# The second up tile of the gated MLP done plainly, and the borders of the MLP stage reordered

## The chip, the cores and the metric

One NeuronCore of one Trainium2 chip runs the whole layer in one launch. The metric is the device time in microseconds (us) of that launch; lower is better. Engines: TensorE (PE, matmuls), VectorE (DVE), ScalarE (ACT), GpSimd (POOL) and SyncE (SP, which here only issues DMAs). Each has a queue of its own that it works off in order; they wait for each other by semaphores.

## The reference

Two groups of tokens (512 and 1024, so 1536 columns) pass through one encoder layer in float32: RMSNorm, one input projection, two kinds of attention, output projection, a gated MLP with a convolution of width 3, a gated embedding, a final RMSNorm. The change touches the border from the output projection to the MLP, the MLP, and the border from its up to its down projection:

```python
h = h + mixed @ w_out[i]
n2 = _rmsnorm(h, ffn_norm[i])
u = _dwconv_centred(n2 @ w_up[i], conv_w[i], conv_b[i])   # up[:, :-2]*w[0] + up[:, 1:-1]*w[1] + up[:, 2:]*w[2] + bias
a, g = jnp.split(u, 2, axis=-1)
h = h + (a * jax.nn.gelu(g, approximate=True)) @ w_down[i]
```

D_MODEL is 1024, D_FF 2816. `w_up` is 1024 x 5632, `w_down` 2816 x 1024.

## The kernel before

Activations lie transposed: features on the 128 partitions, the 1536 tokens along the free axis, in G = 3 groups of 512 columns. `H` holds the residual stream as KT = 8 pieces of 128 features. A float32 product is done in three passes: each operand is split into a rounded high half (`NH`, `WH`, `AH`, by ScalarE) and the rest (`NL`, `WL`, `AL`, by VectorE), and `three_pass` (L317) multiplies high x high, high x low and low x high into one PSUM bank. So each k step of 128 features against 512 tokens is three matmuls of 128x512.

**Stage 3, output projection** (`s3_*`, L1484 to L1757). Eight output tiles, each for three groups. VectorE merges the two halves of a tile's result into `H` (`merge`, L1687: four instructions), ScalarE squares it, GpSimd adds the square to `rstd_h` (L1517). For the last tile this closes the norm of a group: `norm_sums` on PE, `group_std` on ScalarE, `group_recip` on VectorE, `norm_row` on PE, a copy by ScalarE into `rstd_h`; after that VectorE multiplies each of the 24 pieces (8 features x 3 groups) by gain and norm (`normed`, L1737), ScalarE rounds it (`high`, L1653), VectorE makes the low half (`low`, L1742). The weights of the first up tile are split before `last_merge(0)`.

**Stage 4, MLP** (`s4_*`). The 22 tiles j of 128 up columns have a content and a gate half each.

- Tile 0 is done plainly on PE, piece by piece, while the pieces are being made: 6 matmuls per piece, with `WH`, `WL`, `gate0_h`, `gate0_l`.
- Tiles 1 to 21 use a Strassen-Winograd scheme on quarters of the content and gate weights (`A11`, `A21`, `A22`, `A12`, 128x512 each, loaded by `load_quarter`) against group 1 and 2, and a plain one for group 0: `PRODUCTS` (L1771) lists 11 products of 12 matmuls, 132 a tile. It needs sums of weight quarters (`weight_sum`, GpSimd, L1897; rounded by `sum_high`, `sum_low`) and four sets of four combinations of pieces of x (GpSimd, L1920, in the order 1, 3, 2, 4; rounded by `combo_high`, L2060, and `combo_low`, L2190, which write into `NH`, `NL` and over `H`). The combinations are made once, piece by piece, as soon as the pieces of group 2 are there. The product P4 of tile 1 is the first that reads them. `combine` (L2219) and `copy` (L2070) put the products together in `u_a` and `u_g`.
- Per tile: `centre` (ScalarE, L2083: middle tap and bias), `taps` (VectorE, L2202: four instructions per half), `gelu` (ScalarE, L2088), `product` (VectorE, L2208), `store_act` (SP: the tile's result to DRAM). The loop of SP has the loads of the next tile's quarters and the store in one order: A21, store of tile j-1, A11, A22, A12.
- The down projection runs three groups x 22 tiles; a tile is 24 matmuls. `down_high` (L2129, L2130) and `down_low` (L2252, L2255) split weights and activations of a tile. `load_down` and `load_act` load them two tiles ahead, as each buffer comes free. At the end of a group VectorE adds the result to `H` (L2279), ScalarE squares it, GpSimd sums; after that all eight pieces are rounded (`NH`, L2170) and their low halves made (`rest`, L2273) for stage 5, before tile 2 of the next group is split. The embedding's input `pT` and two weight tiles (`PLE_raw`) are loaded right before the loads of tile 4 of group 0, and eight loads of `H` follow tiles 5, 7, ... 19.

Of the kernel before, what the change touches and what calls it, by code (L numbers as in the profile page):

```python
# [105 lines left out]
def build(nc, a):  # L106
    ctx = ExitStack()
    with ctx:
# [134 lines left out]
        S_first = over("S_first", X0, [2, GT], F32, 26 * KB)  # L243
# [1360 lines left out]

        def s3_scalar(act):
# [67 lines left out]
            high(1, range(6, KT))  # L1673
            high(2, range(KT))

        def s3_vector(dve):
# [45 lines left out]
            split_lo(dve, FF0, 0)  # L1722
            dve.wait_ge(w_hi, FF0 + 2)
            for half in range(2):
                low = nc.vector.tensor_tensor(gate0_l[half][:], raw[:, 1, cols(half)], gate0_h[:, cols(half)].bitcast(F32), ALU.subtract)
                if half:
                    low.then_inc(w_lo, 1)

            def last_merge(g):
                last_out_ready(dve, g)  # L1730
                merge(i, 1, g)
# [33 lines left out]
        A11, A21, A22, A12 = range(4)  # L1765
        A_ORDER = [A21, A11, A22, A12]
# [6 lines left out]
        NPROD = len(PRODUCTS)  # L1773
# [8 lines left out]
        def products(j, x):  # L1782

            return (j - 1) * NPROD + (x + 1)

        def copied(j, x):

            return j * 4 + (x + 1)

        def combined(j, x):  # L1790

            return j * 5 + (x + 1)
# [33 lines left out]
        def s4_sync(sp):  # L1826
# [12 lines left out]
            with sp.Fori(1, LAST_J) as j:  # L1839
# [20 lines left out]
            store_act(LAST_J)  # L1860
            load_down(0, 3)
            load_act(0, 3)
            sp.wait_ge(prod, products(LAST_J, X_P3))
            sp.wait_ge(m_st, 16 * NJ)
            nc.sync.dma_start(rstd_h[:], a["pT"][0:P, :]).then_inc(p_ld, 16)
            for x in range(2):
                nc.sync.dma_start(PLE_raw[:, x, :], a["w"][PLE_ROW + x]).then_inc(p_ld, 16)
            for g in range(G):
                for j in range(4 if g == 0 else 0, NJ):
                    load_down(g, j)  # L1870
                    load_act(g, j)
                    if g == 0 and j % 2 == 1 and j < 4 + 2 * KT:
# [6 lines left out]
        def s4_pool(pool):  # L1879
            pool.sem_inc(combo, 5)  # L1880
            pool.sem_inc(u_copy, 2)

            def weight_sum(j, x):
                for q in ((A21, A22), (A11,), (A11, A21), (A12,))[x]:
                    pool.wait_ge(aq_ld[q % 2 ^ (q // 2)], quarter_landed(j, q))
                first = isinstance(j, int) and j == 1
                if first:
                    pool.wait_ge(h_acc, NTILE + 1) if x == 0 else None
                    pool.wait_ge(w_done, FF0)
                else:  # L1890
                    pool.wait_ge(prod, products(j - 1, (X_P5, X_P6, X_P7, X_P3)[x]))
                if x % 2:
                    pool.wait_ge(s_sum, (j - 1) * 4 + (1 if x == 1 else 2))
                out = [S_first if first and y < 2 else S_raw for y in range(4)]
                one, two, op = [(A_raw[:, A21, :], A_raw[:, A22, :], ALU.add), (out[0][:, 0, :], A_raw[:, A11, :], ALU.subtract),
                                (A_raw[:, A11, :], A_raw[:, A21, :], ALU.subtract), (A_raw[:, A12, :], out[1][:, 1, :], ALU.subtract)][x]
                nc.gpsimd.tensor_tensor(out[x][:, x, :], one, two, op).then_inc(s_sum, 1)  # L1897

            for x in range(4):
                weight_sum(1, x)  # L1900
            for n in T_ORDER:
                for k in range(HALF):
                    out = raw_combo(n, k)
                    if n == 1:
                        pool.wait_ge(n_n, 2 * KT + k + 1)
                        pool.wait_ge(n_lo, KT + k + 1)
                        one, two = H[:, k, cols(2)], H[:, k, cols(1)]
                    elif n == 3:
                        pool.wait_ge(n_n, 2 * KT + HALF + k + 1)
                        pool.wait_ge(n_lo, 2 * KT + k + 1)  # L1910
                        one, two = H[:, HALF + k, cols(2)], H[:, k, cols(2)]
                    elif n == 2:
                        pool.wait_ge(n_lo, 2 * KT + HALF + k + 1)
                        pool.wait_ge(t_sum, HALF + k + 1)
                        one, two = H[:, HALF + k, cols(2)], raw_combo(1, k)
                    else:
                        pool.wait_ge(n_lo, KT + HALF + k + 1)
                        pool.wait_ge(t_sum, 2 * HALF + k + 1)
                        one, two = H[:, HALF + k, cols(1)], raw_combo(2, k)
                    nc.gpsimd.tensor_tensor(out, one, two, ALU.subtract).then_inc(t_sum, 1)  # L1920
            with pool.Fori(2, NJ) as j:
# [17 lines left out]
        def s4_tensor(pe):  # L1939
# [18 lines left out]
            pe.wait_ge(st_ok, ROW4 + G)  # L1958

            def product(j, x):  # L1960
# [3 lines left out]
                if kind == "s":  # L1964
                    pe.wait_ge(s_lo, (j - 1) * 4 + (part + 1))
                if x in (X_A11, X_A21):
                    pe.wait_ge(u_copy, copied(j - 1, C_A if x == X_A11 else C_GATE))
# [742 lines left out]
```

## Time and profile before

| | us |
|---|---|
| median of 3 runs | 2158.82 (2158.05 to 2160.03) |
| profiled execution, its own time | 2159.34 |
| its span, first to last instruction | 2157.3 |
| PE busy | 2066.3 (96% of the span) |
| VectorE, ScalarE, GpSimd busy | 1311.2, 883.1, 370.5 |
| mean granted clock of TensorE | 0.983 of full |

The profile is of one execution. A busy time counts an engine's instructions; an engine that waits is idle, and an arrow names what released it. PE's matmuls overlap, so the step from one start to the next says how fast it goes, not the length of one. Times in the rows count from the start of the span: the last tile of the output projection ends near 892, up tile 0 runs from 895 to 941, tile 1 from 941 to 981, the loop over the others to 1582, the down projection's group 0 to 1710, group 1 to 1838.

### The profile page before, as it was taken

Reading aid. Unit: us, or ns where it says so; the run is one execution under the profiler, and the core shown is the slowest. Engines: PE = TensorE matmul, PEld = TensorE weight load, DVE = VectorE, ACT = ScalarE, POOL = GpSimd, SP = SyncE. Lnnn points to the kernel's source line nnn. Section 1 sums busy time; section 2 is a strip of 40 time slices with the busy share of each in tenths; the row PEclk is TensorE's granted clock in tenths of the full one; section 3 lists DMA queues with packets and bytes.
Section 4 is the critical chain, followed back from the end, with each engine's and each line's share of the span. In section 5 each row is a group of like instructions: output and inputs, shape, how many; then the busy total and the mean of one; then the engine's idle time right before and its main releaser. Section 6 shows DMA issues by size and latency. Waiting matters only on the chain.

```text
span 2157.3 us, 29518 instructions
## 1 busy us (share of the span) xinstructions
PE 2066.3 (96%) x10362; PEld 1670.7 (77%) x10362; DVE 1311.2 (61%) x1818; ACT 883.1 (41%) x1491; POOL 370.5 (17%) x252
## 2 busy tenths in 40 slices
PE   8999999999989999979999999999999999999996
PEld 6788887777767788757888888888878788787885
DVE  6799635777766766796555665556644433434546
ACT  6323114666666721254433434334423422423223
POOL 4122201000021233251211122111200100102101
PEclk9999999999999999999999999999999999999998
DMA  5233348101178241202121111211155444341103
GB/s 180 77 128 134 145 151 202 30 15 29 19 164 179 58 185 58 88 5 69 63 65 67 63 49 63 67 64 63 48 205 201 164 146 153 114 143 57 40 30 117
DMA packets 82110, 210.27 MB, mean 97 GB/s; under 512 B 26368, under 2 KB 26752, under 8 KB 82048
## 3 DMA queue, kind: packets, MB, share of 16 engines
q1 hardware_dynamic: 81184, 208.34, 30.3%
q10 hardware_dynamic: 864, 1.13, 0.1%
q8 instruction: 35, 0.57, 0.1%
q14 instruction: 27, 0.22, 0.0%
HBM read 154.39 MB, written 55.05 MB: 97 GB/s over the span
## 4 chain that ended last, share of the span: by engine, by line
PE 76%; DVE 11%; issue 7%; ACT 2%; DMA 2%; POOL 1%; SPq 0%; DVEq 0%; ACTq 0%; POOLq 0%
PE ps L318 21%; PE ps L319 21%; PE ps L320 21%; PE ps L1183 4%; PE ps L1154 3%; PE ps L1137 2%; PE ps L1138 2%; DVE qstd L734 1%; DVE H L1737 1%; DVE qt L747 1%; DVE NL L1742 1%; DMA NH<-act 1%; PE ps L1168 1%; DMA KL<-qkl 0%; DVE H L2471 0%
## 5 line engine op out<-in xcount | busy, mean ns | idle before, releaser
L318 PE MATMUL ps<-NH,WH 128*128 128x512 f32 x840 | 336.1, 400 | 23.0 <-DVE WL L717 9.4
L319 PE MATMUL ps<-NL,WH 128*128 128x512 f32 x840 | 331.8, 395 | 0.0
L320 PE MATMUL ps<-NH,WL 128*128 128x512 f32 x840 | 331.5, 395 | 0.0
L318 PE MATMUL ps<-NL,NH 128*128 128x512 f32 x528 | 208.9, 396 | 15.1 <-DVE NH L2255 11.5
L318 PEld LDWEIGHTS ps<-NH,WH 128*128 128x128 f32 x840 | 160.7, 191 | 63.8 <-DVE NL L1742 12.4
L319 PE MATMUL ps<-NH 128*128 128x512 f32 x528 | 207.8, 394 | 0.0
L320 PE MATMUL ps<-NL 128*128 128x512 f32 x528 | 207.5, 393 | 0.0
L2252 DVE TENSOR_TENSOR NL<-raw,NH 128x1024 fp32r<-128x1024 f32 x66 | 80.8, 1224 | 208.3 <-ACT NH L2129 208.2
L318 PE MATMUL ps<-NH,AH 128*128 128x512 f32 x504 | 196.3, 389 | 2.8 <-DVE AL L2176 2.7
L320 PE MATMUL ps<-NH,AL 128*128 128x512 f32 x504 | 196.1, 389 | 0.0
L319 PE MATMUL ps<-NL,AH 128*128 128x512 f32 x504 | 196.1, 389 | 0.0
L320 PEld LDWEIGHTS ps<-NH,WL 128*128 128x128 f32 x840 | 160.6, 191 | 34.5
L319 PEld LDWEIGHTS ps<-NL,WH 128*128 128x128 f32 x840 | 160.9, 191 | 32.3
L2129 ACT ACTIVATE NH<-raw 128x1024 fp32r<-128x1024 f32 x66 | 69.9, 1059 | 235.6 <-PE ps L320 207.2
L1348 DVE TENSOR_REDUCE nmax<-ps 128x1 f32<-128x1024 f32 (+1 forms) x96 | 100.2, 1044 | 62.7 <-PE ps L1138 62.3
L318 PEld LDWEIGHTS ps<-NL,NH 128*128 128x128 f32 x528 | 100.5, 190 | 38.2 <-DVE NH L2255 13.7
L1897 POOL TENSOR_TENSOR S_raw<-A_raw 128x512 f32<-128x512 f32 x41 | 53.5, 1304 | 406.1 <-PE ps L320 379.7
L1254 ACT ACTIVATE PR<-ps,nmax 128x1024 f32<-128x1024 f32 (+1 forms) x96 | 93.4, 973 | 66.4 <-DVE nmax L1348 64.9
L320 PEld LDWEIGHTS ps<-NL 128*128 128x128 f32 x528 | 100.5, 190 | 21.4
L319 PEld LDWEIGHTS ps<-NH 128*128 128x128 f32 x528 | 100.7, 191 | 21.0
L2219 DVE TENSOR_TENSOR u_a<-u_a,ps 128x512 f32<-128x512 f32 x42 | 28.7, 683 | 140.7 <-PE ps L320 140.7
L318 PEld LDWEIGHTS ps<-NH,AH 128*128 128x128 f32 x504 | 94.6, 188 | 23.2 <-issue 3.6
(246 smaller groups left out, 4234.0 us busy)
## 6 DMA issues: line engine op xcount, KB each, us to landing
raw<-in_w SPq DMA_DIRECT2D x102, 512.0 KB, 3.3
A_raw<-in_wu SPq DMA_DIRECT2D x84, 256.0 KB, 2.7
act<-ca SPq DMA_DIRECT2D x22, 768.0 KB, 3.3
NH<-act SPq DMA_DIRECT2D x66, 256.0 KB, 3.4
xst<-in_xT SPq DMA_DIRECT2D x24, 256.0 KB, 3.2
H<-in_xT SPq DMA_DIRECT2D x8, 768.0 KB, 8.9
H<-hT SPq DMA_DIRECT2D x8, 768.0 KB, 6.3
out_yT<-H SPq DMA_DIRECT2D x24, 256.0 KB, 2.1
```

The costliest lines, as they stand in the source:

```text
L318: nc.tensor.matmul(out, wh, xh, start=first, stop=False, skip_group_check=onto)
L319: nc.tensor.matmul(out, wh, xl, start=False, stop=False, skip_group_check=onto)
L320: return nc.tensor.matmul(out, wl, xh, start=False, stop=last, skip_group_check=onto)
L1137: nc.tensor.matmul(out, q, KH[kind][s][:, k0 + c0:k0 + c0 + n].bitcast(F32R), start=True, stop=False)
L1138: mm = nc.tensor.matmul(out, q, KL[kind][s][:, k0 + c0:k0 + c0 + n].bitcast(F32R), start=False, stop=True)
L1154: mm = nc.tensor.transpose(ps[0:kn, TBANK + b, cols(j, P)], src, ident[:, :])
L1183: mm = nc.tensor.matmul(ps[cols(kb % 2, DH), PVBANK, at:at + queries], VA[s][0:kn, k0 // P + kb, :], PA[0:kn, (m // 2) % 2, n, c0:c0 + que ...
L1254: nc.scalar.activation(probs(m, w), src, ACT.Exp, bias=nmax[:, m:m + 1], scale=-1.0, accum_out=rsum[:, m:m + 1]).then_inc(e_done, 1)
L1348: nc.vector.tensor_reduce(nmax[:, m:m + 1], score_bank(m, w), AXX, ALU.min).then_inc(m_done, 1)
L1897: nc.gpsimd.tensor_tensor(out[x][:, x, :], one, two, op).then_inc(s_sum, 1)
L2129: nc.scalar.activation(NH[:, 2 * s:2 * s + 2, cols(g)], raw[:, s, :].rearrange("p (a n) -> p a n", a=2), ACT.Copy).then_inc(w_hi, 1)
L2252: nc.vector.tensor_tensor(NL[:, 2 * s:2 * s + 2, cols(g)], raw[:, s, :].rearrange("p (a n) -> p a n", a=2), NH[:, 2 * s:2 * s + 2, cols(g) ...
```

## The change

Four things, in stages 3 and 4.

1. Stage 3: `last_merge(0)` comes before the split of the first up weights, `group_recip(0)` before `last_merge(1)`. The rounding of the quarters of tile 1 moves to ScalarE's queue between the pieces of groups 1 and 2, their low halves to VectorE's queue in and behind group 2.
2. Tile 1 is done plainly: four quarters x three groups x 12 matmuls = 144. GpSimd makes no weight sums for it, and makes the combinations of x only when all 24 pieces are done (`n_lo`), then the weight sums of tile 2. The scheme starts with tile 2, and so do the loops.
3. ScalarE and VectorE get a new order for tiles 0 and 1 (below), SyncE one for the quarters of tile 2 and the store of tile 0.
4. Down projection: tile 2 of group 0 is split before `gelu(LAST_J)` and between the taps; the loads of tile 3 go ahead of the last store; `pT` and `PLE_raw` are loaded behind tiles 6, 8 and 10, their rounding moves to tiles 15 to 17; tile 2 of groups 1 and 2 is split during the squares of the group before, and the roundings for stage 5 (`rounded`, `rest`) follow tiles 3 and 4 of the next group.

```diff
@@ s3_scalar
             high(1, range(6, KT))
+            for q in PLAIN_ORDER:                 # [A21, A22, A11, A12]
+                part_high(act, 1, q)
             high(2, range(KT))
@@ s3_vector
-            split_lo(dve, FF0, 0)  ... (gate0_l, w_lo)
             last_merge(0)
+            first_weights_low()                   # the same instructions
+            group_recip(dve, CALL4, 0)
             last_merge(1)
-            group_recip(dve, CALL4, 0)
...
+                if x == 2 * KT + 3:
+                    part_low(dve, 1, A21)
+            for q in PLAIN_ORDER[1:]:
+                part_low(dve, 1, q)
@@ s4_sync
-            with sp.Fori(1, LAST_J) as j:
+            for x, q in enumerate(PLAIN_ORDER):
+                sp.wait_ge(prod, x + 1)
+                load_quarter(sp, 2, q)
+                if q == A11:
+                    store_act(0)
+            with sp.Fori(2, LAST_J) as j:
...
             load_act(0, 2)
-            store_act(LAST_J)
             load_down(0, 3)
             load_act(0, 3)
+            store_act(LAST_J)
             sp.wait_ge(prod, products(LAST_J, X_P3))
-            sp.wait_ge(m_st, 16 * NJ)
-            nc.sync.dma_start(rstd_h[:], a["pT"][0:P, :]).then_inc(p_ld, 16)
-            for x in range(2):
-                nc.sync.dma_start(PLE_raw[:, x, :], a["w"][PLE_ROW + x]).then_inc(p_ld, 16)
             for g in range(G):
                 for j in range(4 if g == 0 else 0, NJ):
                     load_down(g, j)
+                    if (g, j) == (0, 6):
+                        sp.wait_ge(m_st, 16 * NJ)
                     load_act(g, j)
+                    if g == 0 and j in (6, 8, 10):
+                        ...                       # pT, PLE_raw 0, PLE_raw 1
@@ s4_pool
+            pool.wait_ge(n_lo, NTILE)
+            for n in T_ORDER:
+                combo_sum(n)                      # the same 16 subtractions, [1, 3, 2, 4]
             for x in range(4):
-                weight_sum(1, x)
-            ... (combinations, each waiting for its pieces)
-            with pool.Fori(2, NJ) as j:
+                weight_sum(2, x)
+            with pool.Fori(3, NJ) as j:
@@ s4_tensor
+            for x, q in enumerate(PLAIN_ORDER):
+                pe.wait_ge(a_lo4, x + 1)
+                for g in range(G):
+                    bank = PLAIN_BANKS["ga"[x // 2]][g]     # g: 7, 6, 0; a: 1, 2, 3
+                    if x % 2 == 0 and bank < 6:
+                        pe.wait_ge(u_copy, 1 if bank < 3 else 2)
+                    for k in range(HALF):
+                        at = (x % 2) * HALF + k
+                        mm = three_pass(ps[:, bank, :], AH[...], AL[...], NH[:, at, cols(g)], NL[:, at, cols(g)], at == 0, at == KT - 1)
+                mm.then_inc(prod, 1)
             for x in range(NPROD):
-                product(1, x)
+                product(2, x)
@@ s4_scalar
+            def plain_copy(x):
+                for g in range(G):
+                    act.wait_ge(prod, 2 * x + 2)
+                    if g == 0:
+                        act.wait_ge(tap, 4 + 4 * x)
+                    ...                           # u_g or u_a [cols(g)] <- ps, then_inc(u_copy, 1)
-            (part_high(1), combo_high(1), sum_high(1), copies of u_g, u_a, combo_high(3), centre(0, 1), combo_high(2), centre(0, 0), combo_high(4), gelu(0))
+            (copies of u_a, u_g, centre(0, 1), centre(0, 0), combo_high(1), combo_high(2), gelu(0), plain_copy(0), part_high(2, A21), centre(1, 1),
+             combo_high(3), combo_high(4), part_high(2, A11), part_high(2, A22), sum_high(2, 0..2), plain_copy(1), centre(1, 0),
+             part_high(2, A12), gelu(1), sum_high(2, 3))
...
             down_high(0, 1)
+            down_high(0, 2)
             gelu(LAST_J)
...
                 for m in range(KT):
+                    if (g, m) == (0, 6):
+                        down_high(1, 2)
                     if (g, m) == (1, KT - 1):
                         group_std(act, CALL5, 0, END_BANKS[0])
+                        down_high(2, 2)
@@ s4_vector
-            (part_low(1), sum_low(1), combo_low(3, 1, 2, 4), taps(0, 1), taps(0, 0), product(0))
+            (taps(0, 1), combo_low(1), combo_low(2), taps(0, 0), product(0), combo_low(3), part_low(2, A11, A21, A22), sum_low(2, 0), combo_low(4),
+             part_low(2, A12), taps(1, 1), sum_low(2, 1), taps(1, 0), product(1), sum_low(2, 2..3))
...
-            taps(LAST_J, 0, range(4))
+            taps(LAST_J, 0, range(2))
+            down_low(0, 2)
+            taps(LAST_J, 0, (2, 3))
             product(LAST_J)
```

In the lists in brackets the second number of `taps` and `centre` is 1 for the gate half, 0 for the content half. `mul_ok` counts the products, `s_sum` the weight sums, `t_sum` the combinations, `prod` the finished products on PE. `combo_low(1)` and `combo_low(2)` wait, besides the rounding, until combination 2 or 4 has read the raw values that they overwrite; `combo_high(3)` and `combo_high(4)` write over `NH` and `NL` of group 2, so they now wait until the third quarter of the plain tile is through on PE.

## Rows read from the trace of the kernel before

**Rows 1.** Waits of PE over the whole span: line, released by: us, times, longest
```profile
PE ps L318 <- DVE NH L2255: 11.5, 4, 6.4
...
PE ps L318 <- DVE NL L1742: 8.0, 9, 1.7
PE ps L318 <- DVE HR L2190: 7.6, 1, 7.6
...
PE ps L318 <- ACT tok_std L1460: 4.4, 2, 3.5
...
PE ps L318 <- DVE AL L2176: 2.7, 1, 2.7
```

**Rows 2.** Windows: us, busy us (count) of PE, PEld, DVE, ACT, POOL, granted clock, DMA, GB/s
```profile
895.00:941.00 46.00, 37.91 (x162) 27.94 (x161) 45.84 (x53) 19.14 (x34) 23.64 (x15) 1.00 0.02 7
941.00:984.00 43.00, 32.59 (x135) 25.95 (x135) 35.46 (x38) 24.67 (x35) 16.41 (x11) 0.92 0.14 43
984.00:1582.00 598.00, 598.00 (x2640) 495.15 (x2639) 357.21 (x443) 232.74 (x297) 105.06 (x76) 1.00 0.19 62
...
962.60:965.80 3.20, 3.19 (x8) 2.55 (x9) 3.20 (x4) 0.00 (x0) 0.00 (x0) 0.50 0.00 0
...
1606.00:1608.00 2.00, 2.00 (x10) 1.51 (x9) 0.00 (x0) 0.80 (x1) 1.12 (x1) 1.00 1.06 423
```

**Rows 3.** Timeline of PE: start us, us, instruction, idle before and releaser
```profile
954.60 0.39 PE L320 MATMUL ps<-NH,AL 128*128 128x512 f32 x1
962.61 0.80 PE L318 MATMUL ps<-NL,AH 128*128 128x512 f32 x1 [7.62 <-DVE HR L2190]
...
1720.51 0.39 PE L320 MATMUL ps<-NL 128*128 128x512 f32 x1
1727.34 0.79 PE L318 MATMUL ps<-NL,NH 128*128 128x512 f32 x1 [6.45 <-DVE NH L2255]
```

**Rows 4.** Timeline of DVE, pieces of up tile 0
```profile
898.28 0.74 DVE L1737 SCALAR_TENSOR_TENSOR H<-H,gains,rstd_h 128x512 f32<-128x512 f32 x1
898.94 0.68 DVE L1742 TENSOR_TENSOR NL<-H,NH 128x512 fp32r<-128x512 f32 x1
899.54 0.68 DVE L1692 TENSOR_TENSOR to<-ps,acc_a 128x512 f32<-128x512 f32 x1
...
928.32 1.77 DVE L1737 SCALAR_TENSOR_TENSOR H<-H,gains,rstd_h 128x512 f32<-128x512 f32 x1
930.02 0.68 DVE L1742 TENSOR_TENSOR NL<-H,NH 128x512 fp32r<-128x512 f32 x1
```

**Rows 5.** Lines L1920 and L1897 of GpSimd: count, duration ns min/median/max
```profile
L1920 POOL TENSOR_TENSOR H<-H x16: 1669/1704/1749, 921.0 to 950.6; 128x512 f32<-128x512 f32 x16
L1897 POOL TENSOR_TENSOR S_raw<-S_raw,A_raw x20: 1291/1300/1300, 979.2 to 1545.7; 128x512 f32<-128x512 f32 x20
```

**Rows 6.** Timeline of DVE before up tile 0
```profile
880.89 0.68 DVE L1692 TENSOR_TENSOR to<-ps,acc_a 128x512 f32<-128x512 f32 x1
...
884.78 0.69 DVE L1692 TENSOR_TENSOR to<-ps,acc_a 128x512 f32<-128x512 f32 x1 [1.16 <-PE ps L320]
...
887.44 0.17 DVE L1464 RECIPROCAL tok_r<-tok_std 128x4 f32<-128x4 f32 x1
892.30 1.42 DVE L1737 SCALAR_TENSOR_TENSOR H<-H,gains,rstd_h 128x512 f32<-128x512 f32 x2 [4.69 <-ACT rstd_h L364]
```

**Rows 7.** Timeline of ACT: four roundings of a combination in one row
```profile
954.82 2.17 ACT L2060 ACTIVATE NL<-H 128x512 fp32r<-128x512 f32 x4
```

**Rows 8.** Timeline of DVE: content taps and product of tile 0
```profile
966.19 3.79 DVE L2202 SCALAR_TENSOR_TENSOR ca<-u_a,convw,ca 128x511 f32<-128x511 f32 x4
970.08 1.76 DVE L2208 TENSOR_TENSOR ca<-ca,cg 128x1536 f32<-128x1536 f32 x1
```

**Rows 9.** Timelines of ACT and SP at tile 3 of the down projection
```profile
1593.42 0.35 SPq L1829 DMA_DIRECT2D act<-ca  x1
...
1599.54 1.06 ACT L2129 ACTIVATE NH<-raw 128x1024 fp32r<-128x1024 f32 x1 [10.06 <-DMA NH<-act]
```

More of the change, by code:

```diff
@@ L1603, in norm_row, with part_high, part_low @@
             rms_spread(pe, CALL4 + g, g, ROW4 + g + 1, 7, ROW4 + g if g else None)
+        A11, A21, A22, A12 = range(4)
+        A_ORDER, PLAIN_ORDER = [A21, A11, A22, A12], [A21, A22, A11, A12]
+        def part_high(act, j, q):
+            act.wait_ge(aq_ld[q % 2 ^ (q // 2)], quarter_landed(j, q))
+            nc.scalar.activation(AH[:, q, :], A_raw[:, q, :], ACT.Copy).then_inc(a_hi4, 1)
+        def part_low(dve, j, q):
+            if isinstance(j, int) and j == 1:
+                dve.wait_ge(a_hi4, PLAIN_ORDER.index(q) + 1)
+            else:
+                dve.wait_ge(a_hi4, (j - 1) * 4 + (A_ORDER.index(q) + 1))
+                dve.wait_ge(s_sum, (j - 2) * 4 + (4 if q == A12 else 3))
+            nc.vector.tensor_tensor(AL[:, q, :], A_raw[:, q, :], AH[:, q, :].bitcast(F32), ALU.subtract).then_inc(a_lo4, 1)
         def s3_scalar(act):
@@ L1721, in s3_vector, with first_weights_low @@
             body(i, (0,))
[L1722 to L1727, printed above, removed]
+            def first_weights_low():
+                split_lo(dve, FF0, 0)
+                dve.wait_ge(w_hi, FF0 + 2)
+                for half in range(2):
+                    low = nc.vector.tensor_tensor(gate0_l[half][:], raw[:, 1, cols(half)], gate0_h[:, cols(half)].bitcast(F32), ALU.subtract)
+                    if half:
+                        low.then_inc(w_lo, 1)
             def last_merge(g):
                 last_out_ready(dve, g)
+                dve.wait_ge(h_up, LAST_C + g)
                 merge(i, 1, g)
@@ L1892, in weight_sum @@
                 if x % 2:
[L1893 to L1897, printed above, removed]
@@ L2118, in s4_scalar @@
                 centre(j, 0)
-                part_high(j + 1, A12)
+                part_high(act, j + 1, A12)
                 gelu(j)
@@ L2219, in combine @@
                 nc.vector.tensor_tensor(out, one, ps[:, bank, :], ALU.add).then_inc(combo, 1)
-            for q in range(4):
-                part_low(1, q)
-            for x in range(4):
-                sum_low(1, x)
-            for n in (3, 1, 2, 4):
-                combo_low(n)
             taps(0, 1, range(4))
+            combo_low(1)
+            combo_low(2)
             taps(0, 0, range(4))
             product(0)
+            combo_low(3)
+            for q in (A11, A21, A22):
+                part_low(dve, 2, q)
+            sum_low(2, 0)
+            combo_low(4)
+            part_low(dve, 2, A12)
+            taps(1, 1, range(4))
+            sum_low(2, 1)
+            taps(1, 0, range(4))
+            product(1)
+            for x in range(2, 4):
+                sum_low(2, x)
             def front(j):
```

184 lines of the change are left out of this document (93 added, 91 removed).

## The prediction

> **What bounds the kernel now.** I read the page first: TensorE (PE) is busy 96% of the span, so the time is matmuls plus PE's idle gaps. Then the waits of PE over the whole span. In the part that the change touches PE waits 8.0 us for the low halves of x (L1742), 7.6 us for the combinations (HR, L2190), 2.7 us for AL, 11.5 us for the down projection's operands (L2255) and 4.4 us for tok_std [rows 1]. Then the windows: PE is busy 37.91 of 46 us in 895 to 941 and 32.59 of 43 in 941 to 984, while from 984 to 1582 it never stops: 2640 matmuls in 598 us, 0.2265 us each. That is my unit of PE work. After a gap the granted clock is 0.50, the 1.2 GHz level, for a while: 8 matmuls in 3.2 us, so a stretch loses 1.4 us [rows 2]. The timeline of PE shows the two large gaps: 954.60 to 962.61 and 1720.51 to 1727.34 [rows 3]. All that the change can win is in these gaps; the 20-odd tiles in the middle stay PE-bound.
>
> **Why PE starves in 895 to 941.** The DVE timeline has both speeds. With GpSimd idle a gain multiply takes 0.66 us start to start and a low half 0.60: 1.26 us a piece. With GpSimd's combinations running the multiply at 928.32 takes 1.70, so a piece is 2.30 [rows 4]. PE needs 6 x 0.2265 = 1.36 us for a piece. Alone DVE keeps up, beside GpSimd it doesn't. Each side waits for the other: GpSimd's subtraction takes 1.67 to 1.75 us there and 1.29 alone [rows 5]. So a DVE instruction of 0.60 and a GpSimd one alternate at 1.70 us a pair: about 1.1 us of GpSimd is added to each DVE instruction that meets one.
>
> The Trainium skill (SBUF - State Buffer, section SBUF: two separate sides) says that the pair of ports is an exclusive lock, held for the whole instruction by whoever starts first. By it a pair would be 0.60 + 1.29 = 1.89 us, not the 1.70 of the rows; 14 such pairs would end 2.7 us later and the time would be 2135. The rows decide for 1.70.
>
> **Part 1, before the up projection.** Now merge 0 of the last output tile stands behind the weight split and starts at 880.89, though its data were there at 884.75 - 5.44 = 879.3 (24 matmuls before group 1's) [rows 2, 6]. The change puts it first: ready at 882.1 instead of 883.6. Square, GpSimd sum, PE sums and the root follow 3.8 us later, reciprocal at 886.0 instead of 887.44. It now stands ahead of merge 1, which therefore ends at 888.8 instead of 887.5; ScalarE's square of it precedes the row copy, so the first multiply comes at 890.1 instead of 892.30. PE's 0.9 us wait for the sum goes, and I take it that the half-clock stretch behind that wait goes too (if not, 1.2 us). First up matmul: 890.1 + 2.2 = 892.4, against 895.05. **2.7 us.**
>
> **Part 2, the first up tile.** GpSimd's 4 weight sums and 16 combinations no longer run beside DVE; only one norm sum does. 24 pieces x 1.36 + 0.9 (norm sums) + 0.7 (two row spreads) + 1.3 (slower first matmuls after a wait) = 35.5 us of PE work. What is late next: merge 2 (2.65 us of DVE inside group 0) holds up piece 5 by 1.6 us, the one contended multiply piece 6 by 0.8. The four AH roundings, now between the groups on ScalarE, cost 4 x 0.52 = 2.1 us ahead of high(2,0) [rows 7]; DVE leads PE by 2 us there, so they hide; without that lead about 1 us shows. AL of A21 is 0.6 us of DVE inside group 2, hidden likewise. New stretch 37.9 us, against 941.07 - 895.05 = 46.0 (46 in the window [rows 2]). **8.1 us**; the plain second tile starts at 930.3.
>
> **Part 3, second tile plain.** It adds 144 - 132 = 12 matmuls, 2.7 us: 32.6 us without the wait for combinations, where the trace has 42.6 (941.07 to 983.66, both waits and the slow stretch in it). So PE would reach the third tile at 963.0. Is that ready? The chain: GpSimd starts its 16 combinations when DVE ends the last piece, 927.0. Three AL subtractions and four taps meet it, then it alternates with 8 low halves. 3 x 1.7, 2 x 1.25 alone, then the taps (3.72 us in all plus 4 x 1.1) up to 942.8, by when ten combinations are done; six more at 1.70 a pair end at 954 and the last low half of combo 2 at 955 [rows 4, 5, 8]. And now the order of the queues counts: DVE has the content taps, the product, combo_low(3) and part_low(2) *behind* combo_low(2). Taps and product: 3.7 + 1.7 + 2 x 1.1 (the weight sums of tile 2) gives mul_ok at 963. ScalarE's centre(1,1) waits for that, and behind it stand combo_high(3), combo_high(4) (2.1 us each, [rows 7]) and the rounding of A11: 963 + 1.6 + 4.2 + 0.5 = 969.4. DVE's low half: 970.1. PE waits **7.1 us** there, and loses 1.4 to 3 us (2 taken) at the low clock after it. 983.66 - 970.15 - 2.0 = 11.5 us is what parts 1 to 3 give together, **so part 3 by itself gives only 0.7**. Bounds for the wait: 0 (combinations at 1.29 with no tap in their way, copies in time) to 13 (every pair 2.1). A12's load stands behind store_act(0) on SyncE's queue, which waits for the same mul_ok; it lands at 967 and is wanted at 975, hidden. The old 2.7 us wait for AL (A11's load behind store_act at 972) goes, since now mul_ok(1) comes at 985.7, just when P1 of tile 2 ends. Dropped: S_first, the split of GpSimd's sums, the waits in weight_sum: nothing on PE's path, nor does the new wait for h_up, true long before.
>
> **Part 4, into the down projection.** Three waits of PE on L2255, 5.1 us together, plus restarts 0.3, plus one half-clock stretch 1.4 and 0.4 of gap ends: 7.2 to 7.6. (a) Tile 2's low half stood behind taps and product. Now it is between the taps: ScalarE rounds when PE ends tile 0 (1587.8), DVE is done at 1591.4, wanted at 1593.5. Price: gelu 3 us and product 1.7 us later, mul_ok at 1595.0. (b) Tile 3's loads were queued on SyncE behind the store, which issued at 1593.42; ScalarE got the data at 1599.54 [rows 9]. Now they go out at 1587.9: ready at 1596.9, wanted at 1598.9. (c) Tile 4 came late as pT, both PLE tiles and H were ahead of it; now only the store is (5.2 us from issue as for tile 3 before): ScalarE at 1601.1, ready at 1603.9, wanted at 1604.4. That is a margin of half a microsecond. The DMA engines moved 423 GB/s at best [rows 2]; from tile 5 on a tile of 5.44 us brings at most 1.57 MB (weights 0.5, act 0.26, H or pT 0.79), 290 GB/s. The embedding's roundings follow their loads to tiles 15 to 17; nothing in this stage waits for them. **7.2 us.** If the cover fails: up to 5.
>
> **Part 5, groups 0 to 1.** The gap 1720.51 to 1727.34 [rows 3] is tile 2 of group 1 behind eight roundings and eight low halves. Moved to tiles 3 and 4 they have 5.44 - 1.7 us of room each and need 2.1 (ScalarE) and 2.4 (DVE). The tile's rounding goes between squares 5 and 6, at 1716.1; DVE meets GpSimd's sums twice and ends near 1721.1, wanted at 1720.7. 6.6 + 1.5 of clock - 0.5 = **7.6 us**. In group 2 the 3.5 us on tok_std stays: its square root keeps its place.
>
> **Sum.** 11.5 + 7.2 + 7.6 = 26.3 us. The profiled execution took 2159.34 with a span of 2157.3; 2131.0 + 2.0 = 2133.0. The median of the runs is 0.5 under the profiled one: **2132.5 us**.
>
> **Rivals.** (A) *Tile 2 has its operands in time*: combinations or copies are faster than 1.70 a pair. For it: the 1.29 alone and that ScalarE is idle for most of it; against: 16 ops never under 1669 ns in the trace [rows 5]. 7.1 + 2 less: 2124. (B) *The down projection waits anyway*: tiles 3 to 5 late on DMA, the store just moved in front of tile 4. For it: the margin of 0.5. Two waits and a slow stretch remain, 5 us: 2137.5. (C) *The pieces stay slow*, since merge 2, the squares or the roundings on ScalarE, not GpSimd, pace DVE. Against: 1.26 at 898 with them running. 8 us of part 2 back: 2140.5. (D) *Slower than before*: the queue order of part 3. All 16 combinations are ahead of the taps, the product and five more steps, so every microsecond on a combination is 16 on PE. It decides from 1.70 + 26.3/16 = 3.35 us each; at 3.6 it would be 2163. The longest of the trace is 1.75.
>
> **How the numbers follow.** Forecast 0.63 (own range 2128 to 2137), A 0.12, B 0.13, C 0.08, D 0.04. 2124 to 2142 leaves out the ends of A and C, and D. Below 0.2% (4.3 us) a measurement of this kernel can't tell a change from none; of B and C together 0.02 may sink that far. Faster 0.94, same 0.02, slower 0.04.
>
> **What would show it.** Right: the multiplies L1737 mostly at 0.75 us, none of GpSimd's combinations beside them; first up matmul near 892, plain tile near 930; one PE wait of about 7 us at the head of the third tile, released by an AL subtraction; no wait on L2255 above 1 us; the 3.5 us on tok_std still there. Wrong: that wait absent or over 13 us, multiplies still at 1.7, waits at tiles 3 or 4 of the down projection, or a low clock long after a gap.

## The result and the profile after

The changed kernel takes 2133.84 us, median of 4 runs (2132.44 to 2135.18), against 2158.89 for the kernel before in the same session: ratio 0.9884, 95% interval 0.9866 to 0.9901. Forecast was 2132.5. Run again in a later session it gave 2129.21 (2128.03 to 2133.59, ratio 0.9859, 0.9842 to 0.9875); the next section shows how far executions of one kernel lie apart. The profiled execution took 2135.18 with a span of 2133.3, so 24.0 us of span are to be found.

PE's waits in the changed kernel first (line, what it waited for: total, times, longest), to set beside [rows 1]:

```profile
PE ps L317 <- DVE AL L1617: 7.7, 1, 7.7
PE ps L317 <- ACT tok_std L1459: 4.4, 2, 3.5
PE ps L317 <- DVE NL L1760: 2.5, 3, 1.4
PE ps L317 <- DVE H L2334: 1.0, 1, 1.0
PE ps L317 <- DVE NH L2308: 0.6, 1, 0.6
```

The 8.0 us for low halves of x are 2.5, the 7.6 for combinations are gone, and of the 11.5 for the down projection's operands 0.6 are left, with 1.0 more for the additions at a group's end (L2334). In their place is one new wait of 7.7 us for AL, the low half of a weight quarter. PE's timeline has it at the head of the third tile, and the others with it:

```profile
893.07 0.47 PE L317 MATMUL ps<-NH,WH 128*128 128x512 f32 x1 [0.49 <-DVE NL L1760]
...
930.33 0.39 PE L317 MATMUL ps<-NH,AH 128*128 128x512 f32 x1
...
970.88 0.79 PE L317 MATMUL ps<-NH,AH 128*128 128x512 f32 x1 [7.75 <-DVE AL L1617]
...
1693.16 0.47 PE L317 MATMUL ps<-NL,NH 128*128 128x512 f32 x1 [1.04 <-DVE H L2334]
1704.90 0.50 PE L317 MATMUL ps<-NL,NH 128*128 128x512 f32 x1 [0.62 <-DVE NH L2308]
1823.20 0.77 PE L317 MATMUL ps<-NL,NH 128*128 128x512 f32 x1 [3.50 <-ACT tok_std L1459]
1956.97 0.50 PE L317 MATMUL ps<-NH,WH 128*128 128x512 f32 x1 [0.90 <-ACT tok_std L1459]
```

The windows to set beside [rows 2] (busy time and instructions of PE, its weight loads, DVE, ACT and POOL, then granted clock, DMA share, GB/s):

```profile
893.00:930.00 37.00, 34.88 (x159) 28.39 (x160) 36.15 (x55) 17.56 (x30) 4.79 (x3) 1.00 0.07 22
930.00:963.00 33.00, 33.00 (x147) 27.10 (x145) 28.61 (x18) 15.40 (x18) 28.47 (x18) 1.00 0.09 25
971.00:978.00 7.00, 7.00 (x22) 5.55 (x23) 6.16 (x10) 4.82 (x8) 0.00 (x0) 0.67 0.00 0
1571.60:1604.00 32.40, 32.31 (x141) 26.13 (x140) 19.26 (x21) 12.43 (x14) 0.00 (x0) 1.00 0.66 245
```

In tile 0 PE is busy 94% of the time (82% before), in the plain tile all of it, while GpSimd works beside it for 28.5 of 33 us. After the 7.75 us wait the clock is at its lower level for eleven matmul steps from 970.88, 0.43 us each in place of 0.23, which lose 2.35 us; then it is full again (0.67 on the average of 971 to 978). Into the down projection PE hardly stops.

Landmarks, step by step against the forecast (us; gains against the kernel before):

| | before | after | gain | forecast |
|---|---|---|---|---|
| first up matmul | 895.05 | 893.07 | 1.98 | 2.7 |
| tile 0, to the first matmul of the second | 46.05 | 37.26 | 8.79 | 8.1 |
| third tile starts; down projection starts | 983.66; 1582.18 | 970.88; 1571.63 | 12.78; 10.55 | 13.5; 11.5 |
| rest, down projection and later | | | 13.4 | 14.8 |
| sum | | | 24.0 | 26.3 |

The second tile of the kernel before starts at 941.10 in PE's timeline, not at 941.07 as the prediction has it.

### The profile page after: what moved, and what is told of

Its sections match the earlier page's. It is cut to its first block, busy times and chain, and to the rows that moved or that the text cites. A ratio compares the mean times of both kernels' runs of the same rounds, so it can differ in the third digit from the quotient of the medians.

```text
span 2133.3 us, 29620 instructions
## 1 busy us (share of the span) xinstructions
PE 2061.7 (97%) x10374; PEld 1671.8 (78%) x10374; DVE 1302.7 (61%) x1809; ACT 882.3 (41%) x1489; POOL 366.8 (17%) x248
## 4 chain that ended last, share of the span: by engine, by line
PE 79%; DVE 9%; issue 7%; ACT 2%; DMA 1%; POOL 1%; SPq 0%; DVEq 0%; ACTq 0%; POOLq 0%
PE ps L317 22%; PE ps L319 22%; PE ps L318 22%; PE ps L1182 4%; PE ps L1153 3%; PE ps L1136 2%; PE ps L1137 2%; DVE qstd L733 1%; DVE qt L746 1%; PE ps L1167 1%; DVE HR L2235 1%; DMA KL<-qkl 0%; DVE H L2528 0%; DVE NL L2305 0%; DMA NH<-act 0%
## 5 line engine op out<-in xcount | busy, mean ns | idle before, releaser
L317 PE MATMUL ps<-NH,AH 128*128 128x512 f32 x528 | 206.5, 391 | 7.7 <-DVE AL L1617 7.7
L318 PE MATMUL ps<-NL,AH 128*128 128x512 f32 x528 | 206.3, 391 | 0.0
L319 PE MATMUL ps<-NH,AL 128*128 128x512 f32 x528 | 206.1, 390 | 0.0
L2305 DVE TENSOR_TENSOR NL<-raw,NH 128x1024 fp32r<-128x1024 f32 x66 | 82.2, 1246 | 200.4 <-ACT NH L2171 200.4
L317 PEld LDWEIGHTS ps<-NH,AH 128*128 128x128 f32 x528 | 99.7, 189 | 28.9 <-DVE AL L1617 8.2
L319 PEld LDWEIGHTS ps<-NH,AL 128*128 128x128 f32 x528 | 99.7, 189 | 20.8
```

The costliest lines, as they stand in the source:

```text
L317: nc.tensor.matmul(out, wh, xh, start=first, stop=False, skip_group_check=onto)
L318: nc.tensor.matmul(out, wh, xl, start=False, stop=False, skip_group_check=onto)
L319: return nc.tensor.matmul(out, wl, xh, start=False, stop=last, skip_group_check=onto)
L2305: nc.vector.tensor_tensor(NL[:, 2 * s:2 * s + 2, cols(g)], raw[:, s, :].rearrange("p (a n) -> p a n", a=2), NH[:, 2 * s:2 * s + 2, cols(g) ...
```

## The stretch that the experiments are compared by

The instructions ahead of the last output tile are the same in all these kernels, yet the first up matmul of kernels with the same part 1 came at 887.5 to 893.1, and within one session at 887.49 (experiment 6) to 892.78 (8). In the windows of the changed kernel the first 100 us are:

```profile
0.00:100.00 100.00, 88.80 (x382) 72.40 (x383) 66.15 (x78) 46.56 (x91) 34.28 (x27) 0.91 0.36 116
```

and in experiment 4, which has the same instructions there:

```profile
0.00:100.00 100.00, 87.41 (x389) 70.50 (x390) 68.11 (x80) 46.92 (x91) 34.41 (x27) 0.95 0.36 116
```

The granted clock is 0.91 against 0.95, and 382 against 389 matmuls are done. That alone doesn't explain the scatter: experiment 3 has 0.91 there too and starts at 889.11, the changed kernel run again has 0.95 and starts at 891.61. The differences are there by the last but one output tile; where they arise was not traced further. The end varies as well: from the head of the embedding stage to the last instruction it is 176.3 to 176.4 us in nine of the twelve profiled executions and 178.1 to 178.2 in three (experiments 1, 5 and 8).

So a median moves by some us for reasons ahead of the change and behind it. Beside each median stands therefore the stretch of the profiled execution from the first up matmul to the matmul that waits 0.90 us for tok_std at the head of the embedding stage: 1956.97 - 893.07 = 1063.9 in the changed kernel. It leaves out part 1. It is one execution each, and not free of scatter either, as the last section shows. All medians of changed kernels are of 4 to 12 runs, those of the kernel before of 4 to 17.

| kernel | median | ratio to before, 95% | stretch | against the changed kernel |
|---|---|---|---|---|
| before | 2158.89 | | 1085.9 | +22.0 |
| changed kernel | 2133.84 | 0.9884 (0.9866-0.9901) | 1063.9 | |
| the same, again | 2129.21 | 0.9859 (0.9842-0.9875) | 1063.8 | -0.1 |
| 1 front only | 2148.20 | 0.9961 (0.9947-0.9975) | 1079.2 | +15.3 |
| 2 down only | 2143.07 | 0.9942 (0.9929-0.9956) | 1072.6 | +8.7 |
| 3 queue order | 2123.92 | 0.9855 (0.9840-0.9869) | 1056.0 | -7.9 |
| 4 combinations early | 2124.63 | 0.9855 (0.9840-0.9870) | 1056.7 | -7.2 |
| 5 held back, no plain tile | 2160.14 | 1.0003 (0.9993-1.0014) | 1087.6 | +23.7 |
| 6 root moved | 2127.09 | 0.9855 (0.9838-0.9873) | 1058.3 | -5.6 |
| 7 pT, PLE loads back | 2138.17 | 0.9902 (0.9886-0.9919) | 1071.8 | +7.9 |
| 8 store back | 2139.98 | 0.9908 (0.9892-0.9925) | 1068.9 | +5.0 |
| 9 three moves | 2117.27 | 0.9810 (0.9794-0.9826) | 1048.3 | -15.6 |

The kernel before had medians of 2157.31, 2158.64 and 2159.38 in the sessions of 1 to 4, of 6 to 8 and of 5 and 9. An interval is some 3.5 us to each side, so single terms are read from the traces and the medians say whether they add up. By the ratios experiments 3, 4 and 6 (0.9855 each) lie 6 us below the changed kernel's first session and 1 us below its second (0.9859): that they are faster rests on their traces. Experiments 7, 8 and 9 are apart from it by their medians too.

## Experiments

**The changed kernel again.**

> The changed kernel as it is, run again beside the next three, since the first up matmul came anywhere from 888.8 to 893.1 us in four profiles with the same instructions ahead of it. If that is how executions differ, its ratio to the kernel before stays near 0.9884 (24 us faster), and its wait at the head of the third tile stays 7.75 us whatever the start. If the changed kernel has itself a slower front, its first up matmul comes near 893 again.

The ratio fell to 0.9859, the first up matmul came at 891.61, the wait at the third tile was 7.73: the stretch repeats to 0.1 us, the time before it doesn't.

**1 (e1_front_only) and 2 (e2_down_only): either half alone.**

```diff
# 1: items 1 to 3 of the change kept, item 4 (parts 4 and 5 of the prediction) undone
# 2: the kernel before, with item 4 alone; its first lines:
+            down_high(0, 2)
             gelu(LAST_J)
...
-            store_act(LAST_J)
             load_down(0, 3)
             load_act(0, 3)
+            store_act(LAST_J)
```

> Only the first border changed (stage 3 order, plain second tile, held combinations); the down projection as before. My theory, two independent borders: the traces put 10.6 us of the 24 here (start of the down projection 1582.18 to 1571.63), so 2148.3 us, PE's wait for an AL subtraction at the third tile 7 to 8 us, and the four waits for the low halves in the down projection (11.5 us) back. Rival, the parts need each other (a tile that comes earlier only waits later at the second border): under 6 us of gain, 2153 or more.

> Only the second border and the group ends of the down projection changed; everything to the end of the up projection as before. Theory: 13.4 us, 2145.5 us, tile 0 of the down projection starts near 1582, no wait there above 1.1 us. Rival, sum not additive: under 9 us, 2150 or more.

Measured 2148.2 and 2143.07, 9.1 and 14.2 us below the kernel before of that session. The halves give 23.3 together, the change 25.1: within the intervals they add up. Each trace also differs in code that its kernel left as it was. In 2 the wait for AL of A11 at the second border was 4.12 us with 1.7 of low clock behind it, where the kernel before had 2.67 and 0.1; in 1 the clock behind tok_std lost 1.3 less than there. So one profiled execution of the kernel before is known to 3 us or so, and the 22.0 in the table with it.

**3 (e3_order): the order of two queues.** The prediction says that the 7 us wait is made by what stands ahead of the content taps and the product.

```diff
 (DVE)   taps(0, 1, range(4))
-        combo_low(1), combo_low(2)
         taps(0, 0, range(4)), product(0)
+        combo_low(1), combo_low(2)
 (ACT)   combo_high(1)
-        combo_high(2), gelu(0)
+        gelu(0), combo_high(2)
```

> The changed kernel, with VectorE's content taps and product of tile 0 put ahead of the low halves of combinations 1 and 2, and gelu(0) ahead of the rounding of combination 2. Queue theory: the 7.7 us wait at the third tile is there because taps, product and with them centre(1, 1), combinations 3 and 4 and A11 stand behind 16 combinations of GpSimd. Then mul_ok comes near 952, A11's low half before 963, the wait goes and with it the 2.4 us at the low clock: 10 us less, 2123.9 us. Rival, GpSimd's port theory: the chain is bound by the shared time of VectorE and GpSimd, whatever the order; the work only swaps places and the wait stays above 5 us: 2131 or more.

PE's row at the head of the third tile in its timeline:

```profile
962.49 0.79 PE L317 MATMUL ps<-NH,AH 128*128 128x512 f32 x1 [3.30 <-DVE AL L1617]
```

and DVE's timeline before it:

```profile
938.38 7.95 DVE L2247 SCALAR_TENSOR_TENSOR ca<-u_a,convw,ca 128x511 f32<-128x511 f32 x4
946.44 2.66 DVE L2253 TENSOR_TENSOR ca<-ca,cg 128x1536 f32<-128x1536 f32 x1
949.02 10.40 DVE L2235 TENSOR_TENSOR HR<-H,HR 128x512 fp32r<-128x512 f32 x8
959.35 2.48 DVE L2235 TENSOR_TENSOR HR<-H,NH 128x512 fp32r<-128x512 f32 x4
961.76 1.88 DVE L1617 TENSOR_TENSOR AL<-A_raw,AH 128x512 fp32r<-128x512 f32 x3
```

The order of the queues made most of the wait: 7.75 has become 3.30. The expectation that it would go was wrong. The product ends at 949.10, 10.6 us sooner than in the changed kernel when both are counted from the first up matmul, and the centre is free as much sooner; but all twelve low halves of combinations 1 to 3 are now between it and AL. The median was as expected by luck: 4.45 of wait and 0.7 of clock come from this border (5.1 us), another 2.75 because the clock didn't fall after the later wait on tok_std, and 2 are scatter outside the stretch (its profiled execution reached the first up matmul 4 us sooner). The rival (a wait above 5 us, whatever the order) is refuted by the trace.

**4 (e4_early): combinations as soon as their pieces are there.** Is holding them back (part 2) what makes the change fast?

```diff
-            pool.wait_ge(n_lo, NTILE)
+            # ahead of each combination: its own two pieces
             for n in T_ORDER:
```

> The changed kernel, but GpSimd makes each combination as soon as its pieces are there, as before the change, so beside VectorE's pieces. Theory: the pieces of group 2 take 2.3 us again instead of 1.36, up tile 0 ends 6 to 7 us later (plain tile near 937), and in return the combinations are done early, the wait at the third tile (7.7 + 2.4 at the low clock) is gone: net 3 to 4 us faster than the changed kernel, 2130 us. Rival, holding the combinations back is what brings the gain: 6 us slower than the changed kernel, 2140 us.

PE's timeline, at three of the eight pieces that it waits for (the changed kernel: three) and at the start of the plain tile:

```profile
918.64 0.50 PE L317 MATMUL ps<-NH,WH 128*128 128x512 f32 x1 [0.54 <-DVE NL L1760]
920.94 0.50 PE L317 MATMUL ps<-NH,WH 128*128 128x512 f32 x1 [0.64 <-DVE NL L1760]
923.90 0.50 PE L317 MATMUL ps<-NH,WH 128*128 128x512 f32 x1 [1.32 <-DVE NL L1760]
...
931.68 0.39 PE L317 MATMUL ps<-NH,AH 128*128 128x512 f32 x1
```

DVE's timeline, at the first multiply that meets a combination:

```profile
911.59 1.79 DVE L1755 SCALAR_TENSOR_TENSOR H<-H,gains,rstd_h 128x512 f32<-128x512 f32 x1
```

and GpSimd's beside it:

```profile
911.15 1.69 POOL L1941 TENSOR_TENSOR H<-H 128x512 f32<-128x512 f32 x1 [12.31 <-DVE H L1755]
```

PE waits at the pieces again, each contended multiply takes 1.77 to 1.79 in place of 0.74, and the plain tile starts 931.68 - 888.80 = 42.9 us after the first up matmul, not 37.3: 5.6 us lost. But seven combinations are done before the last piece, no wait is left at the third tile (its 7.75 and 2.35 of clock are gone), and 2.7 us more come off later, most of it at two waits of the down projection (1.0 for L2334 gone, 1.2 less of clock behind tok_std). The stretch is 7.2 us shorter than the changed kernel's, 4.5 of it from this border. So with the plain tile in place and the change's queue order holding back is a loss, by the trace; the median can't tell it from the changed kernel's second session. The rival was right about the cost at the pieces, and wrong about the whole.

**5 (e5_hold_only): held back, without the plain tile.** One line, `pool.wait_ge(n_lo, NTILE)`, ahead of the combinations of the kernel before.

> The kernel before, with one line added: GpSimd makes the combinations only when the low halves of all 24 pieces are done. No plain second tile, no other reordering. My theory: the pieces speed up as in the changed kernel (tile 1 starts about 5.4 us sooner), but the combinations then run behind them with only the 48 matmuls of the plain products as cover, 10.9 us against 27 us of combinations: PE's wait for them ends near 966 where it ended at 962.6, so the whole is 3 to 4 us slower than the kernel before. Rival: holding them back is itself what makes the changed kernel faster, with or without the plain tile: 8 us faster than before.

From the list of PE's waits:

```profile
PE ps L318 <- DVE HR L2191: 14.5, 1, 14.5
PE ps L318 <- DVE NL L1742: 4.4, 3, 1.7
```

Tile 0 took 40.0 us instead of 46.0, and the wait for combinations 14.5 instead of 7.6: same time within the interval, stretch 1.7 longer. Neither size was right (3 to 4 slower, 8 faster), but the mechanism of the first theory was: the wait moved. It ended 68.25 us after the first up matmul, where it had ended 67.56 after it, and 1.1 us more were lost at the low clock. So without the plain tile the 6.0 us that the pieces gain are paid back, and 1.8 more.

**6 (e6_std): the root of group 0's final norm.**

```diff
-                    if (g, m) == (1, KT - 1):
+                    if (g, m) == (1, 2):
                         group_std(act, CALL5, 0, END_BANKS[0])
```

> The root of the final norm of group 0 is taken on ScalarE behind square 2 of group 1 in place of behind square 6. My theory: the prediction left this wait alone because the step kept its place; the root stands at 1822.80 behind seven squares that come at the pace of VectorE and GpSimd, and it is all that PE waits for at 1823.20. Moved, it is done near 1818.5, PE wants it at 1819.7: the wait of 3.5 us and the 2.75 us of low clock behind it go, 6.2 us less than the changed kernel. Rival: PE then waits at the same place for the low half or the sums that come later, at most 1 to 2 us less.

ScalarE's timeline; in the changed kernel the root stood at 1822.80, 7.2 us later than here when both are counted from the first up matmul:

```profile
1808.74 1.28 ACT L1459 ACT_TABLE_LOAD   x1
1810.03 0.26 ACT L1459 ACTIVATE tok_std<-ps,misc 128x4 f32<-128x4 f32 x1
```

PE's wait there is 0.58 us, for another operand, with full clock after it. Stretch 5.6 shorter (expected 6.2); the median is 2.1 below the changed kernel of the same session, less than the trace says and inside what two such intervals allow. That the root's place makes the wait is shown by the trace, what it is worth in the median is not.

**7 (e7_loads) and 8 (e8_store): the two moved loads of part 4.**

```diff
# 7
+            sp.wait_ge(m_st, 16 * NJ)
+            (loads of pT, PLE_raw 0, PLE_raw 1)    # as in the kernel before
             for g in range(G): ...                 # load_down, load_act from tile 4 on
# 8
+            store_act(LAST_J)
             load_down(0, 3)
             load_act(0, 3)
-            store_act(LAST_J)
```

> The changed kernel with pT and the two PLE weight tiles loaded ahead of tile 4 again, behind the wait for the last store. My theory, part 4(c) of the prediction: by the rows of the kernel before, tile 4's data reached ScalarE 13.8 us after the store was issued (1607.20 - 1593.42) and PE started 3.0 us later. The store is issued at 1584.6 now, so tile 4 can start at 1601.4 and PE wants it at 1593.7: a wait of 7.7 us and 1.5 us of low clock, 9 us slower than the changed kernel. Rival: with the tile 3 loads gone ahead, the DMA engines are free enough that the order of the loads costs nothing (0 to 1 us).

> The changed kernel with the last store ahead of the loads of tile 3 again. My theory, part 4(b): the store waits for the last product, so tile 3's loads are issued at 1585 and not at 1577; in the kernel before the data reached ScalarE 6.1 us after the store, so 1590.7, ready at 1593.7, wanted at 1588.3. A wait of 5.4 us and 1.5 us of low clock, 6.5 to 7 us slower than the changed kernel. Rival: only the 1.6 us that PE waited there before, since tile 2's split is what made it late: 1.6 to 3 us slower.

PE's timeline in 7, at tile 4:

```profile
1595.51 0.79 PE L317 MATMUL ps<-NL,NH 128*128 128x512 f32 x1 [5.89 <-DVE NH L2305]
```

and in 8, at tile 3:

```profile
1593.61 0.80 PE L317 MATMUL ps<-NL,NH 128*128 128x512 f32 x1 [5.31 <-DVE NH L2308]
```

In 8 the wait is 5.31 (expected 5.4), with 1.54 of clock. In 7 it is 5.89 and 2.15 of clock, 8.0 together (expected 9): tile 4's data came 12.3 us after the store was issued, not 13.8. The medians are 9.0 and 10.8 us above the changed kernel of the same session, the stretches 7.9 and 5.0 (in 8 the clock behind tok_std lost 1.4 less, the end took 1.9 longer, and the rest of the difference to its median is not accounted for). Both rivals, 0 to 1 and 1.6 to 3 us, are refuted. In the kernel before PE waits less at each of these tiles:

```profile
1595.18 0.50 PE L318 MATMUL ps<-NL,NH 128*128 128x512 f32 x1 [1.56 <-DVE NH L2255]
1602.52 0.50 PE L318 MATMUL ps<-NL,NH 128*128 128x512 f32 x1 [1.59 <-DVE NH L2255]
1610.17 0.50 PE L318 MATMUL ps<-NL,NH 128*128 128x512 f32 x1 [1.92 <-DVE NH L2255]
```

A late tile gives the next one time to arrive, so undoing one edit alone costs more than its own wait there; that reading fits the rows, but no run tests it by itself.

**9 (e10_best): three moves that the experiments point to.** Experiments 3 and 6, and AL of A11 ahead of the last six low halves.

```diff
# VectorE's queue against experiment 3, abridged
-            combo_low(1), combo_low(2), combo_low(3)
-            part_low(2, A11), part_low(2, A21), part_low(2, A22)
+            combo_low(1), combo_low(2, first two)
+            part_low(2, A11)
+            combo_low(2, last two), combo_low(3)
+            part_low(2, A21), part_low(2, A22)
```

> The changed kernel with three moves: taps and product of tile 0 on VectorE, and gelu(0) on ScalarE, ahead of low halves and roundings of combinations as in e3_order; the low half of A11 of tile 2 between the second and third low half of combination 2 (in e3_order it stood behind twelve of them and PE waited 3.30 us for it and lost 1.7 us of clock); and the root of group 0's final norm as in e6_std. My theory: the wait at the head of the third tile is gone or below 0.5 us, the one on tok_std too. From the changed kernel's stretch of 1063.9 us between the first up matmul and the head of the embedding stage come off 7.75 + 2.35 and 6: 1048, and the time is 15 to 16 us below it, 2115 to 2118 us. Rival: VectorE can't make the remaining low halves in the 48 matmuls of cover that the plain products give, and a wait of 2 to 5 us comes at the fifth or sixth product of tile 2: 2119 to 2122 us.

From the list of PE's waits:

```profile
PE ps L317 <- DVE NL L1760: 2.5, 3, 1.4
PE ps L317 <- DVE AL L1617: 1.2, 1, 1.2
PE ps L317 <- DVE NH L2311: 1.0, 2, 0.7
PE ps L317 <- ACT tok_std L1459: 0.9, 1, 0.9
```

2117.27 us (2115.75 to 2122.12), ratio 0.9810, stretch 1048.3, 15.6 us below the changed kernel's, as its first theory had it; by the ratios it is 11 (against the second session of the changed kernel) to 16 us faster. What is left at the border is 1.17 us for the low half of the next quarter, at 964.68, behind the low halves of combination 3.

## Why the prediction was right

The new wait, its releaser and its place in the trace came as forecast, and the gaps that were to close did. The terms missed by 0.1 to 1.5 us each, in both directions, so a median 1.3 us from the forecast is luck in part; the second session was 3.3 below it. The multiplies L1737 are L1755 in the changed kernel, the low halves L1742 are L1760, and L2255 is L2305 and L2308.

**Tile 0 (8.1, came 8.79).** As worked out, the contention of GpSimd was the cause: experiment 5, which holds back only the combinations, gets 6.0 of it. The other 2.8 go with GpSimd's four weight sums, which met VectorE's instructions in the kernel before, and with the new order of the queues; no run separates the two. In the groups by line of the window 893 to 930 the 22 multiplies have a mean of 788 ns:

```profile
L1755 DVE SCALAR_TENSOR_TENSOR H<-H,gains,rstd_h 128x512 f32<-128x512 f32 x22 | 17.3, 788 | 0.0
L1760 DVE TENSOR_TENSOR NL<-H,NH 128x512 fp32r<-128x512 f32 x23 | 15.7, 683 | 0.8 <-ACT NH L1667 0.5
```

One took 1.78, the one that met GpSimd's norm sum, and the waits at pieces 5 and 6 (1.41 and 0.65 us) are the two that were named.

**Before it (2.7, came 1.98).** Counted from the merge of group 1 of the last but one output tile, behind the scatter of the start, it is 2.18. DVE's timeline in the kernel before and in the changed one:

```profile
868.46 0.69 DVE L1692 TENSOR_TENSOR to<-ps,acc_a 128x512 f32<-128x512 f32 x1 [2.17 <-PE ps L320]
...
868.66 0.69 DVE L1708 TENSOR_TENSOR to<-ps,acc_a 128x512 f32<-128x512 f32 x1 [2.17 <-PE ps L319]
```

From there to the first up matmul it is 26.59 and 24.41 us, and 26.56 to 26.59 in the three profiled kernels without part 1, 24.39 to 24.41 in the nine with it: this term is known to 0.03 us. The step that missed is the norm sum of group 1: it ran at 889.63 for 1.30 us and met the first two multiplies, which the prediction counts uncontended. DVE's timeline:

```profile
890.07 2.06 DVE L1755 SCALAR_TENSOR_TENSOR H<-H,gains,rstd_h 128x512 f32<-128x512 f32 x2 [1.19 <-ACT rstd_h L363]
892.23 0.69 DVE L1760 TENSOR_TENSOR NL<-H,NH 128x512 fp32r<-128x512 f32 x1
```

The first multiply was at 890.1 as forecast; the two took 2.06 us where [rows 6] has 1.42, and the low half behind them started 2.16 us after the first one's start, against 1.51 before. That is the 0.6 us. The half-clock stretch ahead of it went, as assumed.

**Second and third tile (0.7, came -0.2).** The chain held link by link. GpSimd's timeline:

```profile
926.88 26.89 POOL L1931 TENSOR_TENSOR H<-H 128x512 f32<-128x512 f32 x16 [23.78 <-DVE NL L1760]
```

DVE's:

```profile
935.07 7.33 DVE L2247 SCALAR_TENSOR_TENSOR cg<-u_g,convw,cg 128x511 f32<-128x511 f32 x4 [4.29 <-ACT cg L2111]
942.33 13.68 DVE L2235 TENSOR_TENSOR HR<-H,HR 128x512 fp32r<-128x512 f32 x8
955.94 5.86 DVE L2247 SCALAR_TENSOR_TENSOR ca<-u_a,convw,ca 128x511 f32<-128x511 f32 x4
961.90 1.76 DVE L2253 TENSOR_TENSOR ca<-ca,cg 128x1536 f32<-128x1536 f32 x1
```

and ScalarE's:

```profile
963.75 1.67 ACT L2111 ACTIVATE cg<-u_g,convb,convw 128x1536 f32<-128x1536 f32 x1 [11.35 <-DVE ca L2253]
965.33 2.17 ACT L2088 ACTIVATE NH<-H 128x512 fp32r<-128x512 f32 x4
967.41 2.17 ACT L2088 ACTIVATE NL<-H 128x512 fp32r<-128x512 f32 x4
969.49 1.13 ACT L1609 ACTIVATE AH<-A_raw 128x512 fp32r<-128x512 f32 x2
```

Combinations ended at 953.8 (forecast 954), combination 2's low halves at 956.0 (955), the product at 963.7 (963), PE started at 970.88 (970.15). Sixteen combinations in 26.89 us are 1.68 each, so the rate of 1.70 a pair stood. The Trainium skill (SBUF - State Buffer, section SBUF: two separate sides) has the pair of ports held for a whole instruction by whoever came first; this trace doesn't agree with the sum of 0.60 and 1.29, which would be 1.89. That more than half of the wait, 4.45 of 7.75 us, came from queue order and not from the combinations' rate, experiment 3 shows. Rival A did not come: at 1.68 the combinations were no faster than counted. Experiments 4 and 9 have the operands in time at the head of the third tile, by another order and not by a faster combination. Rival D shares the mechanism; at 1.68 it stayed far from its price.

**Down projection (14.8, came 13.4).** No wait at tiles 2, 3 and 4 of group 0; part 4 gave 7.1 of its 7.2 us. Tile 4's operands were ready and wanted at 1593.8, so the margin of half a microsecond was zero, and Rival B missed by that. What fell short is group 0 to 1, 6.1 of 7.6; no experiment has it alone. ScalarE's timeline has tile 1's data late:

```profile
1689.49 1.06 ACT L2171 ACTIVATE NH<-raw 128x1024 fp32r<-128x1024 f32 x1 [5.09 <-DMA NH<-act]
```

Its load was issued at 1684.30, so it took 5.2 us, where the median of this transfer is 3.4. DVE made tile 1's low half first, and the group's additions (L2334) behind it kept PE 1.04 us. That wait is not a fixed price: it was 0.48 when the same kernel ran again, 1.15 in experiment 1, which has the old code there, and none in 2 and 4. Tile 2's operands cost another 0.62 where I had 0.5. The wait on tok_std stayed at 3.5, as predicted.

**What the prediction did not see.** It priced part 2 and the wait of part 3 as separate terms. They are one: seven combinations made early cost 5.6 us at the pieces and save 10.1 at the third tile (experiment 4). The forecast of the time was right, but reading part 2 as a pure gain was wrong, and so was pricing the plain tile at 0.7. From the first up matmul to the start of the down projection it is 687.1 us in the kernel before (690.2 in experiment 2, the same code there), 690.6 with the combinations held back alone (5), 678.6 in the changed kernel and 673.9 with the plain tile and the combinations early (4). So the gain comes with the plain tile, whose 32.6 us of matmuls cover the combinations (kernel 4 has the new queue orders too, and no run separates the two), and holding the combinations back gives 4.6 of it away again.

## What to carry to other kernels

Work that is taken off a contended stretch has to end somewhere: follow it to its last reader and through each queue that it stands in, and price the two places together. When a new wait appears, look first at what stands ahead of its releaser in the in-order queues; here one exchange in two queues was worth 5 us of the trace at its border and three moves 15.6 of the stretch. Count a point of the trace from a landmark right ahead of the change, not from the start of the span: the starts here differ by up to 5.6 us. Compare small terms by a stretch of the trace that begins behind the scatter, look whether the untouched waits in it came out alike, and use medians for the sum.

## What the runs showed of the hardware

The same wait can cost different amounts afterwards. The wait on tok_std was 3.4 to 3.8 us in all ten profiled executions whose kernels have it; the matmul steps after it, against 0.2265 us each, lost 2.8 us (changed kernel), 2.9 (the same again), 3.0 (the kernel before), 2.7 (7), 1.7 (1, 2, 4 and 5), 1.5 (8) and 0.1 in 3, whose PE timeline shows a matmul at full speed right away:

```profile
1814.12 0.47 PE L317 MATMUL ps<-NL,NH 128*128 128x512 f32 x1 [3.41 <-ACT tok_std L1459]
```

The wait of 7.7 us at the third tile lost 2.3 to 2.8 in all six executions that have it. The wait at tile 4 of the down projection, the third of three short ones, lost 1.7 in the kernel before after 1.92 us, and 0.1 in experiment 5 after 1.69. What decides between them these runs don't show. This spread, the start that comes up to 5.6 us apart, and the end with its 1.9 us are what limits a comparison of medians.

A VectorE instruction with two operands in SBUF that meets a GpSimd subtraction takes about 1.05 us longer, whichever it is: a multiply 1.79 in place of 0.74 (experiment 4), four taps 7.95 in place of 3.79 (3 and the kernel before).
